# Attention taken by pairs of slots: the values of one pair of slots between the scores of the next pair's two slots

## The reference, cut to what matters

```python
s = jnp.einsum('brqhd,brkwhd->bhrqkw', qg, kg).astype(jnp.float32) * ATTN_SCALE
s = s + bias[None].astype(jnp.float32)
p = jax.nn.softmax(s.reshape(B, H, rows, GRID_W, kh * GRID_W), axis=-1)
o = jnp.einsum('bhrqkw,brkwhd->brqhd', p, vg)
...
g = jax.nn.sigmoid((h @ w_branch_gate).astype(jnp.float32)).astype(x.dtype)
merged = g_a * (o_a @ w_branch_a) + g_b * (o_b @ w_branch_b) + g_c * (o_c @ w_branch_c)
```

## Time and profile before

| | |
|---|---|
| three executions, median | 3094.06 us (3092.19 to 3097.15) |
| span of the profiled execution | 3092.8 us |
| PE busy | 3032.8 us, 98% of the span |
| DVE busy | 1683.1 us, 54% |
| ACT busy | 1205.3 us, 39% |
| POOL busy | 288.2 us, 9% |

### The profile page before, as it was taken

One profiled execution on the slowest core, in us unless ns is written; L12 is line 12 of the kernel. 1 busy time (PEld: TensorE's weight loads), 2 busy tenths in 40 slices (PEclk: granted clock), 3 DMA queues, 4 the chain that ended last, 5 costly groups with the idle time before them and its releaser, 6 DMA issues.

```text
span 3092.8 us, 40119 instructions
## 1 busy us (share of the span) xinstructions
PE 3032.8 (98%) x15272; PEld 2463.6 (80%) x15272; DVE 1683.1 (54%) x3050; ACT 1205.3 (39%) x2238; POOL 288.2 (9%) x344
## 2 busy tenths in 40 slices
PE   8999999999999999999999999999999999999998
PEld 7888887788888888778678888888778768888887
DVE  6653364446565426656756555436556766555434
ACT  4322334443432224644543322224545553322223
POOL 0000110001100012011001000013111001100002
PEclk9999999999999999999999999999999999999999
DMA  5333373225233233225125223334224315322332
GB/s 172 111 96 114 109 148 125 92 88 178 92 102 100 93 108 110 81 100 163 69 73 173 96 96 97 95 110 142 91 91 132 116 39 182 104 96 96 99 99 96
DMA packets 105999, 338.18 MB, mean 109 GB/s; under 512 B 15360, under 2 KB 15888, under 8 KB 105680
## 3 DMA queue, kind: packets, MB, share of 16 engines
q1 hardware_dynamic: 84816, 272.45, 27.4%
q0 software_dynamic: 20992, 63.15, 6.8%
HBM read 299.24 MB, written 27.52 MB: 106 GB/s over the span
## 4 chain that ended last, share of the span: by engine, by line
PE 90%; ACT 3%; DVE 3%; issue 2%; DMA 1%; POOL 0%; SPq 0%; POOLq 0%; DVEq 0%; ACTq 0%
PE bk L1655 26%; PE bk L1657 26%; PE bk L1656 26%; PE bk L1731 3%; PE bk L1753 2%; PE bk L1739 2%; ACT t L1893 1%; PE bk L1694 1%; PE bk L1695 1%; PE bk L1696 1%; DVE t L1974 1%; ACT t L1901 1%; ACT t L1841 0%; DVE t L2124 0%; PE bk L1707 0%
## 5 line engine op out<-in xcount | busy, mean ns | idle before, releaser
L1655 PE MATMUL bk<-t,t 128*128 128x512 f32 x3784 | 1483.5, 392 | 20.4 <-DVE t L1974 12.5
L1657 PE MATMUL bk<-t,t 128*128 128x512 f32 x3784 | 1469.7, 388 | 0.0
L1656 PE MATMUL bk<-t,t 128*128 128x512 f32 x3784 | 1468.1, 388 | 0.0
L1655 PEld LDWEIGHTS bk<-t,t 128*128 128x128 f32 x3784 | 712.8, 188 | 170.1 <-issue 19.7
L1657 PEld LDWEIGHTS bk<-t,t 128*128 128x128 f32 x3784 | 712.5, 188 | 147.0
L1656 PEld LDWEIGHTS bk<-t,t 128*128 128x128 f32 x3784 | 713.4, 189 | 141.6
L1974 DVE TENSOR_TENSOR t<-t,t 128x1024 fp32r<-128x1024 f32 (+3 forms) x538 | 615.6, 1163 | 370.2 <-ACT t L1841 369.7
L1841 ACT CAST t<-t 128x1024 fp32r<-128x1024 f32 (+3 forms) x538 | 513.6, 983 | 221.9 <-PE bk L1657 118.7
L1884 ACT CAST t<-t 128x512 fp32r<-128x512 f32 x88 | 54.7, 622 | 433.5 <-DVE t L2034 433.5
L1893 ACT ACTIVATE t<-t,t 128x256 f32<-128x256 f32 (+3 forms) x336 | 173.9, 519 | 123.0 <-DVE t L2047 122.4
L2280 POOL TENSOR_TENSOR t<-t,t 128x512 f32<-128x512 f32 x58 | 78.3, 1350 | 1387.0 <-ACT t L1871 1387.0
(11 more groups left out here) (173 smaller groups left out, 2008.7 us busy)
## 6 DMA issues: line engine op xcount, KB each, us to landing
t<-in_f_g SPq DMA_DIRECT2D x88, 512.0 KB, 4.3
t<-in_f_u SPq DMA_DIRECT2D x88, 512.0 KB, 3.5
t<-in_f_d SPq DMA_DIRECT2D x64, 512.0 KB, 4.4
t<-in_gate SPq DMA_DIRECT2D x48, 512.0 KB, 3.6
gate_scratch<-t POOLq DMA_DIRECT2D x64, 256.0 KB, 2.3
t<-gate_scratch POOLq DMA_DIRECT2D x64, 256.0 KB, 3.9
t<-in_f_d SPq DMA_DIRECT2D x32, 384.0 KB, 3.1
t<-in_wo SPq DMA_DIRECT2D x24, 512.0 KB, 3.7
```

The source lines that it names most:

```text
L1655: pe.matmul(o, wh, xh, start=start, stop=False)
L1656: pe.matmul(o, wh, xl, start=False, stop=False)
L1657: return pe.matmul(o, wl, xh, start=False, stop=stop)
```

## The change

`attend` now goes by pairs of slots. For every pair it does, in this order: the turns of both slots of the pair before, what waits in `behind`, the score of the new pair's first slot, the values of both slots of the pair before, the score of the new pair's second slot, the norm of its first and of its second slot, and then the units' `post` and `pre` and one fill. The copy of the turned probabilities goes back into the slot's own tile of scores, so `PTr` is gone and `Sr` has six tiles, which are freed by the last value (`gone`). The tables of fills have one entry per pair, with the same fills in the same order. What follows a slot's value (`done`) stands behind the norm of the new pair's first slot, or right behind the value with `at_once`.

```diff
-        self.Sr = Ring([t([128, T], RA + (78 + 2 * i) * K) for i in range(3)] + [t([128, T], o + 18 * K)])
-        self.PTr = Ring([t([128, T], RA + (84 + 2 * i) * K) for i in range(2)])
+        self.Sr = Ring([t([128, T], RA + (78 + 2 * i) * K) for i in range(5)] + [t([128, T], o + 18 * K)])
...
-    def attend(self, slots, fill=()):
+    def attend(self, slots, fill=(), at_once=False):
...
-        for s in range(n + 2):
-            if 0 <= s - 2 < n:
...
-                k = self.step("turn", bs=bs)
...
+        pairs = [range(i, min(i + 2, n)) for i in range(0, n, 2)]
...
+        def turn(s):
+            bs = []
+            for X in st_[s]:
+                b, bank, bt = self.PB.take()
+                X["b"] = b
+                bs.append(dict(bank=bank, bt=bt, S=X["S"], w=X["w"], p=X["p"], PT=X["S"]))
+            k = self.step("turn", bs=bs)
+            for j, X in enumerate(st_[s]):
+                self.PB.give(X["b"], (k, "a", j))
+                X["p"] = (k, "a", j)
...
+        def between(ss):
+            for f in ss:
+                for B in slots[f]:
+                    for U in B:
+                        if U.get("post"):
+                            U["post"]()
+            for f in ss:
+                for B in slots[f]:
                     for U in B:
                         if U.get("pre"):
                             U["pre"]()
...
+            for f in next(fill, None) or ():
+                f()
+
+        for p in range(len(pairs) + 1):
+            old = pairs[p - 1] if p else ()
+            new = pairs[p] if p < len(pairs) else ()
+            for s in old:
+                turn(s)
+            self.turned()
+            back, self.behind = self.behind, []
+            for f in back:
+                f()
+            if not new:
+                between(())
+            for s in new[0:1]:
+                score(s)
+            for s in old:
+                for X in st_[s]:
+                    self.Sr.give(X["i"], X["gone"])
+            for s in old:
+                value(s)
+            for s in new[1:2]:
+                score(s)
+            for s in new[0:1]:
+                norm(s)
+            for s in old if not at_once else ():
+                done(s)
+            for s in new[1:2]:
+                norm(s)
+            if new:
+                between(new)
...
-        self.attend(self.batches(na_us), [[ga[at[i]]] if i in at else None for i in range(10)])
+        self.attend(self.batches(na_us), [ga[0:2], ga[2:3], ga[3:4], ga[4:6], ga[6:7]])
...
-        self.attend(self.batches(us), self.portions(opened4[60:96], (0, 4) + (1, 1, 2) * 6 + (2, 1, 3, 2)))
+        self.attend(self.batches(us), self.portions(opened4[60:96], (4, 3, 3, 3, 3, 3, 3, 3, 3, 3, 3, 2)))
...
-                e.wait_ge((n, "pe", j), b["f"])
+                e.wait_ge((n, "pe", j))
```

More of the change, by code:

```diff
@@ new lines, in turn, with score @@
+        def turn(s):
[8 more added lines that the diff above has]
+                X["p"] = (k, "a", j)
+        def score(s):
+            bs = []
+            for X, B in zip(st_[s], slots[s]):
+                b, bank, bt = self.PB.take()
+                i, S, f = self.Sr.take()
+                o_ = 0
+                ws = []
+                for U in B:
+                    U["at"] = o_
+                    ws.append(dict(at=o_, w=U["w"], q=U["q"](), k=U["k"](), qk=U["qk"](), table=U["table"], tt=U.get("tt"),
+                                   scale=U["scale"], init=U.get("init", BIG), nm=U["nm"], sm=U["sm"]))
+                    o_ += U["w"]
+                assert o_ <= 512
+                extra = B[0]["extra"](B) if B[0].get("extra") else None
+                bs.append(dict(bank=bank, bt=bt, S=S, f=f, ws=ws, extra=extra))
+                self.names += 1
+                X.update(S=S, i=i, w=o_, b=b, gone=("gone", self.names))
+            k = self.step("score", bs=bs)
+            for j, (X, B) in enumerate(zip(st_[s], slots[s])):
+                for U in B:
+                    if U.get("after"):
+                        U["after"]((k, "pe", j))
+                X["es"] = [(k, "e", j, i) for i in range(len(B))] + ([(k, "x", j)] if bs[j]["extra"] else [])
+                self.PB.give(X["b"], (k, "m", j, len(B) - 1))
@@ new lines, in value @@
+        def value(s):
+            bs = []
+            for X, B in zip(st_[s], slots[s]):
+                vs = []
+                for U in B:
+                    if U.get("open"):
+                        U["open"]()
+                    vs.append(dict(v=U["v"](), o=U["o"](), vt=U["vt"](), ot=U["ot"](), at=U["at"], add=U.get("add", False)))
+                bs.append(dict(PT=X["S"], p=X["p"], vs=vs, gone=X["gone"]))
+            k = self.step("value", bs=bs)
+            for X in st_[s]:
+                X["k"] = k
+            if at_once:
+                done(s)
@@ new lines, in done, with norm @@
+        def done(s):
+            for j, (X, B) in enumerate(zip(st_[s], slots[s])):
+                for i, U in enumerate(B):
+                    if U.get("done"):
+                        U["done"]((X["k"], "pe", j, i), X["es"])
+        def norm(s):
+            for X, B in zip(st_[s], slots[s]):
+                nh = len(B)
+                gate = B[0]["gate"](nh) if B[0].get("gate") else None
+                k = self.step("norm", S=X["S"], at=[U["at"] for U in B] + [X["w"]], es=X["es"], sm=B[0]["sms"](nh),
+                              rs=B[0]["rss"](nh), gate=gate)
+                X["p"] = (k, "d")
@@ L1275, in layer @@
         opened4 = self.quarters("gate" + s_, range(24), H)
[L1276 to L1277 removed]
+        self.attend(self.batches(us), [opened[0:1], None, opened[1:2], None, opened[2:3], opened[3:4], opened[4:5]])
         fr = self.now()
@@ L1755, in tensor @@
                         if end:
-                            e.then_inc(ins, "values", (n, "pe", k, i))
+                            e.then_inc(ins, "values", (n, "pe", k, i), *([b["gone"]] if i == len(b["vs"]) - 1 else []))
         elif kind == "dil_out":
```

27 lines of the change are left out of this document (6 added, 21 removed).

## The result

The changed kernel takes 3101.02 us (median; 3096.48 to 3103.95) beside 3095.76 us for the kernel before (3092.19 to 3097.89) on the same chips: ratio 1.0017, 95% interval 1.0011 to 1.0024. It is slower, by 5 us where 24 us less were forecast (3094 to 3070 us), and so outside the range; measured to that precision it is not "no change", though it lies within my bound of 0.2%. Two executions of the experiments, one with the tanh behind the copies (3388 us) and one with the windows in order (5093 us), ran in a slower state with a granted clock of 0.85 and 0.56, and the ratios leave them out. In all functions of the engines the lines stand 36 further down: scores L1767, turns L1775, values L1789, dense matmuls L1691 to L1693, ScalarE's copies L1937 and exponentials L1929, the head's copies L1969, VectorE's peaks L2083.

The account below looks back on a forecast made before the run. TensorE, busy 98% of a 3092.8 us span, was taken as the bound. Less 13.7 us slack and 10.3 us waits (26.1 removed, 15.8 new), plus 1.3 us from span to time: 3070 us; 8-in-10 range 3055 to 3087 us.

Parts of the forecast that it names:

- my bound of 0.2%: Whole kernel: faster or slower means by more than 0.2% (6.2 us), about what a measurement can tell.
- Slack: TensorE in the attention stretches: merged stretches leave fewer seams between kinds of work, 13.7 us less.
- Value to score: TensorE's new seam from values to scores: 0.18 us each, 39 seams, up to 7.0 us more or less gain.
- (a): Norm before turn on VectorE: about no wait, but 0.5 us per compressed softmax in sparse attention, 3 us in both layers.
- SP and POOL have the same order of transfers: Transfer queues: order unchanged, so transfers were costed at nothing.
- (b) Gates in PB: Neighbourhood and latent attention: tanh ahead of ScalarE's copies delays scores 0.65 us per such pair; 3.1 and 4 us.
- all 26.1 us: TensorE's waits in the ten attention stretches before the change: all depend on rearranged places and were counted as removed.
- (c) Heads: Latent attention: the wait for a projected head's copies moves from a score to a turn, 1.9 us per layer, 3.8 us.
- The step from span to time: Whole kernel: the median of timed runs lies 1.3 us above the span, taking 3068.8 to 3070 us.
- ScalarE's copies take the gain: Copies delayed in all 51 pairs by 0.65 us: 37 us of new waits, 3091 us, no change; chance 0.09.
- my own forecast: Whole kernel: new waits of 0 to some 22 us, time 3058 to 3077 us; chance 0.57.
- costs at nothing: Score tiles, ScalarE's exponentials, weights' casts (two units ahead of use) and transfer order: no added time.

Follow-up runs that it names:

- all four edits: Changed kernel plus compressed softmax behind turns, tanh behind copies, windows in order, last latent block in PB, and neighbourhood gate blocks in PB: 3070.11 us, ratio 0.9923.
- The first experiment: Changed kernel with the sparse attention's next compressed scores and softmax written behind the next iteration's turns: 3088.12 us, ratio 0.9977 to the kernel before.

## Why the prediction was wrong

**Slack: right in sum.** I forecast 13.7 us less. In the kernel without half clock it is 13.7 us. In the changed kernel only 633.5 + 2.7 - 632.1 = 4.1 us show, because half clock adds to busy time there. What it adds is read from the same stretches at full clock: 2.6 us in each sparse attention (118.2 against 115.6 us), 1.6 us in the second latent attention (74.9 against 73.3 us in the first) and 2.2 us in the neighbourhood attention (64.6 against 62.5 us), 9.0 us together. 4.1 + 9.0 = 13.1 us. Value to score at 0.18 us was the right middle value: in the kernel with all four edits two slots' values take 1.89 us to the score behind them (478.23 to 480.12 us), 0.19 us more than the 1.70 us of my estimate. That the sum fits to the tenth is partly luck. Added up from start to start over the ten stretches, less the waits (an estimate from the timelines of both kernels, good to about 1 us in all), fills fell by 8.7 us (7.7 forecast), values by 7.1 (8.5), scores by 3.8 (2.1) and small pieces by 1.3 (none forecast), and the turns grew by 8.4 us, not 4.6: the errors cancel. The estimate with the Trainium skill's drain ("TensorE: Matmul & The Clock Gate", Part 2), 53 ns at each of 120 changes of mode, would have been 6.4 us (a time of 3077 us, not the 3078 that I wrote); the trace has more than twice that.

**Waits put in, (a): the step that failed.** "In the sparse attention three times per layer the compressed softmax stands between norms and the next peaks, some 3 us on VectorE; I put 0.5 us of wait for each: 3 us in both layers." Measured: 6.7 us of wait in the first layer (3.16 + 2.39 + 1.15) and as much in the second, 13.4 us in both layers where I had put 3. I followed the chain on VectorE only and forgot that one operation of it runs on ScalarE, whose queue is in order: the exponential stood ahead of the pair's four copies, idle until VectorE had done four norms and three operations of the chain. The first experiment takes this away and gains 13 us; the one with the chain ahead of the norms shows that both together made it, exponential ahead of copies and chain behind norms. The norms themselves were as forecast: turns wait for them by at most some tenths in the changed kernel.

**No term for the transfers.** "SP and POOL have the same order of transfers" is true, but the second slot's values are needed some 4 us sooner, and the loads landed no sooner: 2.6 us of wait in this run, 2.7 to 4.8 us in others with the same order of slots.

**(b) Gates in PB: right in size, incomplete.** Forecast 0.65 us for each, measured 0.75 us three times in the neighbourhood attention (I had four) and 0.63 and 0.75 us in each latent one (I had three); a third wait there, 0.73 us, stands behind the copies of a head and no tanh, and a fourth is 0.38 us. Missing was the last block of the latent attention behind the output split, 2.77 us in place of 1.08 us, twice. The trace of before had this wait; I took all 26.1 us of it as removed.

**(c) Heads: moved, not gone, as forecast,** but 2.00 + 0.69 us per layer at the turns instead of 1.9. Of the 39.2 - 15.8 = 23.4 us of waits above the forecast, the softmax is 10.4 us, the last block 5.5, the transfers 2.6 and the heads 1.6; the rest is the balance of small ones.

**No term for the clock.** Around waits of 2.3 and 3.2 us the granted clock was 0.66 and 0.77 in the two stretches printed above. That is 9 us of 3100, more than a quarter of what was lost on the forecast.

**The step from span to time.** I added 1.3 us to the span, from the median of three executions. In every execution whose span is on record the time is 1.8 or 2.2 us above its span, so 0.5 to 0.9 us of the miss lie here.

**The rivals.** "ScalarE's copies take the gain" came nearest (37 us of new waits and 3091 us, against 39.2 us and 3101 us measured), and its condition, "something stands ahead of them", is what happened, but in 19 places with a few large waits and not in every pair. I gave it 0.09. The range under my own forecast, 3058 to 3077 us, is new waits of 4 to 23 us, not of 0 to 22 us as written. The kernel with all edits, at 3070 us with 17.5 us of waits, is near the case that I forecast (15.8 us); the change as written was not that kernel. What I had called costs at nothing (weights' casts) stood: the cast of 1.03 us between exponential and copies only mattered behind the late exponential.

## What to carry to other kernels

When steps are reordered, follow every operation of a moved chain on **each** engine that it visits, and ask for each in-order queue what now stands directly ahead of what the bounding engine waits for. Write down for every transfer and every bank when it is needed after the change, and not only whether its place in the queue is the same. If a reordering that should gain does not, look for the few longest waits: here nine places (six of the softmax, one of value tiles, two of the last block) held 21.5 us of wait, 9 us more were lost to the clock, and after a few small edits the forecast gain was there.

## What the hardware showed unexpectedly

The half clock did not follow from a wait with certainty: with the same 7.1 us of waits a sparse attention was busy for 116.8 us in the run with the windows in order (0.99, first row below) and for 118.2 us in that of the changed kernel (0.97), and the last wait of the latent attention, 2.77 us in both layers, was followed by low clock in the second alone (1.00 from 1332 to 1338 us, 0.62 from 2285.88 to 2290 us). The kernel before had one such piece too, behind a wait of 1.8 us outside the attention (second row; window, length, busy, granted clock), while the same wait in the first layer was followed by full clock (1.00 from 1242 to 1251 us):

```profile
1491.61:1615.56 123.95, 116.84 (x903) 0.99 0.15 52
```
```profile
2192.00:2203.00 11.00, 9.17 (x35) 0.84 0.30 93
```

Part of the spread between runs of one kernel may be this. The changed kernel's 18 runs lie within 7.5 us, the five of the kernel with all four edits within 1.2 us, and the mean granted clock of a run goes with its time: 0.998 in the changed kernel's fastest run and 0.994 in its slowest. No experiment tested it by itself.
